# Sample attention of a hybrid decoder step: cached keys and values in ten tiles per sequence in place of twelve

## The reference, cut to what matters

```python
DILATED = ((128, 1), (512, 4), (2048, 16))

def dilated_attention_sample(q, kc, vc):          # kc, vc: 2048 cached rows, then 8 new ones
    W = kc.shape[1] - T
    for window, dil in DILATED:
        j = jnp.arange(window // dil + 1)
        idx = W + ti[:, None] - dil * j[None, :]
        ...                                       # scores, softmax, product with the values
        outs.append(o / den[..., None])
        lses.append(mx[..., 0] + jnp.log(den))
    return combine_by_denominator(outs, lses)     # weights exp(lse), so one softmax over all three sets
```

## Time and profile before

| | before |
|---|---|
| median of 3 runs | 2793.16 us (2788.93 to 2793.80) |
| span of the profiled execution | 2790.8 us |
| matrix engine busy in the span | 2667.3 us, 96% |
| VectorE, ScalarE, GpSimd busy | 65%, 39%, 25% |
| sample stage, first PE instruction to the end of its last value product | about 1077 to 1246 us |

### The profile page before, as it was taken

How to read it: one execution, slowest core, us unless ns; L and a number is a source line. 1 busy time by engine, 2 the same in 40 slices (tenths; PEclk the granted TensorE clock), 3 DMA queues, 4 the chain that set the end, 5 groups by cost and what they waited for, 6 DMA issues and landing times. The chain is left out here.

```text
span 2790.8 us, 45736 instructions
## 1 busy us (share of the span) xinstructions
PE 2667.3 (96%) x17331; PEld 2256.3 (81%) x17331; DVE 1806.6 (65%) x3848; ACT 1075.5 (39%) x1975; POOL 692.4 (25%) x585
## 2 busy tenths in 40 slices
PE   7999999999899998989989999899999999999997
PEld 6888888878777776768877888799998888778886
DVE  6722566333688885567667676755655766887778
ACT  4312332010566774333346555555553211221113
POOL 1167212120245453112210000100002434333332
PEclk9999999999999999989999999999999999999999
DMA  5367543254454547967846777778869777786672
GB/s 184 140 214 265 198 145 143 107 178 139 138 174 155 172 142 290 399 263 261 303 164 209 269 270 269 263 269 298 278 234 335 271 243 255 265 310 225 220 266 87
DMA packets 342705, 628.68 MB, mean 225 GB/s; under 512 B 38431, under 2 KB 241315, under 8 KB 326742
## 3 DMA queue, kind: packets, MB, share of 16 engines
q1 hardware_dynamic: 273132, 530.24, 54.8%
q10 hardware_dynamic: 68218, 91.51, 9.1%
q0 software_dynamic: 1152, 4.19, 0.4%
HBM read 455.36 MB, written 237.61 MB: 248 GB/s over the span
## 5 line engine op out<-in xcount | busy, mean ns | idle before, releaser
L3573 DVE TENSOR_TENSOR mlp_acc<-mlp_acc,bank 128x512 f32<-128x512 f32 x440 | 299.6, 685 | 143.4 <-PE bank L2861 137.1
L2859 PE MATMUL bank<-mlp_wd,mlp_u_hi 128*128 128x512 f32 x896 | 350.5, 391 | 8.9 <-DVE mlp_acc L3573 5.1
L2861 PE MATMUL bank<-mlp_wd,mlp_u_lo 128*128 128x512 f32 x896 | 349.2, 390 | 0.0
L2860 PE MATMUL bank<-mlp_wd,mlp_u_hi 128*128 128x512 f32 x896 | 349.1, 390 | 0.0
L3342 ACT ACTIVATE mlp_u_hi<-mlp_u_raw 128x768 fp32r<-128x768 f32 x126 | 113.1, 945 | 445.4 <-POOL mlp_u_raw L3210 445.0
L2859 PE MATMUL bank<-mlp_h_hi,mlp_wu_hi 128*128 128x272 f32 x896 | 259.3, 289 | 9.3 <-DVE mlp_h_lo L3431 4.8
L2860 PE MATMUL bank<-mlp_h_lo,mlp_wu_hi 128*128 128x272 f32 x896 | 258.8, 289 | 0.0
L2861 PE MATMUL bank<-mlp_h_hi,mlp_wu_lo 128*128 128x272 f32 x896 | 257.9, 288 | 0.0
L292 PE MATMUL p_bank<-p_w_hi,p_hT_hi 128*128 128x512 f32 x640 | 250.4, 391 | 5.2 <-DVE p_stage L836 5.1
L294 PE MATMUL p_bank<-p_w_hi,p_hT_lo 128*128 128x512 f32 x640 | 249.1, 389 | 0.0
L293 PE MATMUL p_bank<-p_w_lo,p_hT_hi 128*128 128x512 f32 x640 | 249.1, 389 | 0.0
(11 more groups left out here) (448 smaller groups left out, 6104.4 us busy)
## 6 DMA issues: line engine op xcount, KB each, us to landing
mlp_wd<-wd SPq DMA_DIRECT2D x31, 2048.0 KB, 8.1
mlp_wd<-wd SPq DMA_DIRECT2D x32, 1536.0 KB, 7.3
mlp_u_raw<-u SPq DMA_DIRECT2D x256, 128.0 KB, 2.4
out_win_k_sample<-in_cache_k SPq DMA_DIRECT2D x48, 680.0 KB, 8.9
out_win_v_sample<-in_cache_v SPq DMA_DIRECT2D x48, 680.0 KB, 9.6
mlp_wu_raw<-in_w_up SPq DMA_DIRECT2D x31, 1024.0 KB, 6.0
p_w_raw<-in_w_tok SPq DMA_DIRECT2D x10, 2048.0 KB
wd<-mlp_un_hi SPq DMA_DIRECT2D x21, 896.0 KB, 4.5
```

The costliest lines, as they stand in the source:

```text
L2859: nc.tensor.matmul(out, ah, bh, start=fresh and k == 0, stop=False, skip_group_check=not fresh)
L2860: nc.tensor.matmul(out, ah, bl, start=False, stop=False, skip_group_check=not fresh)
L2861: ins = nc.tensor.matmul(out, al, bh, start=False, stop=k == n - 1, skip_group_check=not fresh)
L3573: v.tensor_tensor(a, a, b[:], ALU.add).then_inc(summed, 1)
```

## The change

Of the last 512 rows only those of residue 8 to 15 are loaded by the second DMA, two tiles in place of four. Partition p = 32a + i gets rows 16i + 8 + 2a and the next one, counted from the start of the last 512 (2 rows, 4 KB in one run; 512 KB in all). The rows of residue 0 to 7 are there once, in the tiles of dilation 16, and the table now counts for every position all three windows. With this the third group has two tiles: two key transposes, a score block of 256 columns, two probability transposes, and the value products have 11 tiles in place of 13. All places in memory stay as large as before (`HOME`).

```diff
-KT = 13
-OLD = 12 * P
+WT = 10
+KT = WT + 1
+OLD = WT * P
 KEYS = OLD + NS
+HOME = 12
...
-    pos = np.concatenate([16 * p + r for r in range(8)] + [WB - 512 + 4 * p + c for c in range(4)]
-                         + [WB + np.arange(DEC_T)])[None, :]
+    late = WB - 512 + 16 * (p % 32) + 8 + 2 * (p // 32)
+    pos = np.concatenate([16 * p + r for r in range(8)] + [late + y for y in range(2)] + [WB + np.arange(DEC_T)])[None, :]
...
-    d16 = (back >= 0) & (back % 16 == 0) & (back <= 2048) & (part16 | new)
-    d4 = (back >= 0) & (back % 4 == 0) & (back <= 512) & ~part16
-    d1 = (back >= 0) & (back <= 128) & ~part16
+    d16 = (back >= 0) & (back % 16 == 0) & (back <= 2048)
+    d4 = (back >= 0) & (back % 4 == 0) & (back <= 512)
+    d1 = (back >= 0) & (back <= 128)
...
 def load_window(sp, dst, cache, b, landed):
     sp.dma_start(dst[:, 0:8], cache[b].rearrange("(i r) c -> i r c", r=16)[:, 0:8]).then_inc(landed, 16)
-    sp.dma_start(dst[:, 8:12], cache[b, WB - 512:WB, :].rearrange("(i r) c -> i r c", r=4)).then_inc(landed, 16)
+    sp.dma_start(dst[:, 8:WT], cache[b, WB - 512:WB, :].rearrange("(i z a y) c -> z a i y c", z=2, a=4, y=2)[1]).then_inc(landed, 16)
...
             def keys(b, ci):
-                for x in (4 * ci + 1, 4 * ci + 3):
+                for x in range(4 * ci + 1, min(4 * ci + 4, WT), 2):
...
             def masked(b, c):
-                w = 512 if c < 3 else NS
+                w = min(512, OLD - 512 * c) if c < 3 else NS
...
             def scores(b, ci):
-                w = 512 if ci < 3 else NS
+                w = min(512, OLD - 512 * ci) if ci < 3 else NS
...
                     if i < 3:
-                        for k in range(4):
+                        for k in range(min(4, WT - 4 * i)):
```

More of the change, by code:

```diff
@@ L1954, in sample_tables @@
     p = np.arange(P)
-    pos = np.concatenate([16 * p + r for r in range(8)] + [WB - 512 + 4 * p + c for c in range(4)]
-                         + [WB + np.arange(DEC_T)])[None, :]
+    late = WB - 512 + 16 * (p % 32) + 8 + 2 * (p // 32)
+    pos = np.concatenate([16 * p + r for r in range(8)] + [late + y for y in range(2)] + [WB + np.arange(DEC_T)])[None, :]
+    assert len(set(pos[0].tolist())) == pos.size
     back = WB + t - pos
     n = OLD + DEC_T
[L1959 to L1962, removed]
-    d16 = (back >= 0) & (back % 16 == 0) & (back <= 2048) & (part16 | new)
-    d4 = (back >= 0) & (back % 4 == 0) & (back <= 512) & ~part16
-    d1 = (back >= 0) & (back <= 128) & ~part16
+    assert pos.shape[1] == n
+    d16 = (back >= 0) & (back % 16 == 0) & (back <= 2048)
+    d4 = (back >= 0) & (back % 4 == 0) & (back <= 512)
+    d1 = (back >= 0) & (back <= 128)
     count = d16.astype(np.float32) + d4 + d1
@@ L1994, in __init__ @@
             if b < DEC_B:
-                order += [("k", b, x) for x in range(12)]
+                order += [("k", b, x) for x in range(WT)]
             if b:
@@ L2087, in mix_sample @@
         assert -(-nc.sbuf_base // 32) * 32 == K.front_at + 4 * TOP
-        sb("kin_home", [P, 12, AW])
-        later = [12 * AW]
+        sb("kin_home", [P, HOME, AW])
+        later = [HOME * AW]
         def front(name, *shape):
@@ L2099, in mix_sample @@
         knT = sb("knT", [P, PAIRS, NS])
-        pr = front("pr", 2, KEYS)
+        pr = front("pr", 2, HOME * P + NS)[:, :, 0:KEYS]
         qs, knew, mq, mkk, n32 = K.qs, K.knew, K.mq, K.mkk, K.n32
         qz = front("qz", DEC_B, PAIRS, QW)
-        pT = front("pT", KT, P)
+        pT = front("pT", HOME + 1, P)
         mask, mask_new = sb("mask", [P, OLD]), sb("mask_new", [P, DEC_B, NS])
@@ L2120, in mix_sample @@
         SC, PV, ML = (3, 4), 5, (6, 7)
-        pT_last = kin[1][:].rearrange("p x c -> p (x c)")[:, 12 * AW - KT * P:].rearrange("p (x r) -> p x r", r=P)
+        pT_last = kin[1][:].rearrange("p x c -> p (x c)")[:, HOME * AW - KT * P:].rearrange("p (x r) -> p x r", r=P)
         def pt(b):
-            return pT[:] if b + 1 < DEC_B else pT_last
+            return pT[:, 0:KT] if b + 1 < DEC_B else pT_last
         def pv(b):
@@ L2168, in _ @@
                 if b + 2 < DEC_B:
-                    sp.wait_ge(s["turned"], T.turned("k", b, 11))
+                    sp.wait_ge(s["turned"], T.turned("k", b, WT - 1))
                     load_k(b + 2)
@@ L2215, in _ @@
             assert own.n == 6
-            pool.wait_ge(s["turned"], T.turned("k", 0, 11))
+            pool.wait_ge(s["turned"], T.turned("k", 0, WT - 1))
             for h in range(MH):
@@ L2235, in rows @@
         def rows(x):
-            return P if x < 12 else NS
+            return P if x < WT else NS
         @block.scalar
@@ L2251, in keys @@
             def keys(b):
-                for x in range(0, 12, 2):
+                for x in range(0, WT, 2):
                     n = 3 * b + x // 4
@@ L2269, in probs @@
                         act.wait_ge(s["summed"], b)
-                    A(pt(b)[:, 4 * i:4 * i + 4], bank[T.bank("p", b, i)][:].rearrange("p (x r) -> p x r", x=4),
+                    w = min(4, WT - 4 * i)
+                    A(pt(b)[:, 4 * i:4 * i + w], bank[T.bank("p", b, i)][:, 0:w * P].rearrange("p (x r) -> p x r", x=w),
                       ACT.Copy).then_inc(s["copied_a"], 1)
@@ L2336, in masked @@
                     dve.wait_ge(s["turned"], T.turned("p", b - 2, 3))
-                table = mask[:, 512 * c:512 * (c + 1)] if c < 3 else mask_new[:, b]
-                v.tensor_tensor_reduce(pr[:, p, 512 * c:512 * c + w], bank[SC[n % 2]][:, 0:w], table, 1.0, 2 * NEG,
+                at = 512 * c if c < 3 else OLD
+                table = mask[:, at:at + w] if c < 3 else mask_new[:, b]
+                v.tensor_tensor_reduce(pr[:, p, at:at + w], bank[SC[n % 2]][:, 0:w], table, 1.0, 2 * NEG,
                                        ALU.add, ALU.max, st[:, p, c:c + 1]).then_inc(s["masked"], 1)
@@ L2465, in keys @@
                 p = b % 2
-                for x in range(4 * ci, 4 * ci + 4):
+                for x in range(4 * ci, min(4 * ci + 4, WT)):
                     dst = open_group("k", b, x)
@@ L2473, in scores @@
                 n = 4 * b + ci
-                w = 512 if ci < 3 else NS
+                w = min(512, OLD - 512 * ci) if ci < 3 else NS
                 if ci < 3:
-                    after(pe, T.out("k", b, 4 * ci + 2))
-                    after(pe, T.out("k", b, 4 * ci + 3))
+                    last = min(4 * ci + 4, WT)
+                    after(pe, T.out("k", b, last - 2))
+                    after(pe, T.out("k", b, last - 1))
                 if n >= 2:
@@ L3760, in sb @@
             return ctx.enter_context(K.nc.sbuf_tensor("shared_" + name, shape, F32))
-        K.k_first, K.k_second = K.place("k_first", 0, [P, 12, AW]), K.place("k_second", TOP, [P, 12, AW])
+        K.k_first, K.k_second = K.place("k_first", 0, [P, HOME, AW]), K.place("k_second", TOP, [P, HOME, AW])
         K.C = sb("C", [P, MH, MD + 1])
```

10 lines of the change are left out of this document (5 added, 5 removed).

## The result

The changed kernel takes 2847.33 us in the median of 4 runs (2846.64 to 2848.36), the kernel before 2791.05 us in 4 runs beside it: a ratio of 1.0214, 95% interval 1.0196 to 1.0233. That is 56 us slower, where I forecast 19.5.

A forecast was written before the change was run, and what follows sets the result against it. Matrix engine bounds the kernel; after the change transfers lead the sample stage. 13 loads x 2.7 = 35.1 us, less 12.0 slack, 1.0 idle and 2.6 back, gives 19.5; 2793.2 + 19.5 = 2812.7 us, range 2787 to 2830.

The forecast's parts named there:

- the mechanism that leads: Sample stage: second parts run on four of 16 DMA engines, so transfers lead the matrix engine; 0.70 for 2799 to 2825 us.
- the tail: Output projection behind the sample stage: starts 19.5 us later and is itself unchanged.
- that sign: In the changed profile, 512 KB parts land 5 us or more behind their 2048 KB parts, where 1024 KB took 2.5.
- the rate: Key and value loads: second part on four engines at 98 GB/s takes 5.3 us; each load grows 2.7 us, 13 loads 35.1.
- slack and idle time: Up to value load 6: 12.0 us between its landing and first use, plus 1.0 us in which the DMA engines were idle.
- C: Rival on the second parts: at 80 GB/s a load grows by 4.0 us, 36 us in all, 2830 us; chance 0.08.
- B: Rival: four engines run faster while twelve idle, second part about 3.7 us; near 2793, 2788 to 2799 us; chance 0.10.
- A: Rival: second parts spread over all 16 engines, matrix engine keeps the lead; 2782.8 us, 2776 to 2786; chance 0.12.
- the engine's saving: Matrix engine in the sample stage: 11.8 us less work, net 10.4; transposes 0.97 and value products 0.47 us a sequence.
- SP's issue: SP's queue: issuing a load grows from 0.43 to 0.68 us, under its waits of 98 us.
- From value products 6 to L1816: End of the sample stage: 7.58 us becomes 5.0, as VectorE's projection preparation is done during the wait; 2.6 us back.
- The lower clock behind a wait: Matrix engine: a lower clock after its new waits costs nothing, since it waits anyway.

The follow-up runs named there:

- 1024 KB on four engines: Kernel before the change, keeping its twelve tiles, with the second part's rows laid out so the source's outermost dimension is 4: 2960.3 us, ratio 1.0625.
- the keys alone: Changed kernel with key second parts kept at outermost dimension 4 and value second parts at outermost dimension 32: 2808.7 us, ratio 1.0086 to the kernel before.
- outermost 32: Changed kernel with partition p = 4i + a and the second part's source outermost dimension 32, not 4, in one DMA: 2773.7 us, ratio 0.9951 to the kernel before.

## Why the prediction was right and wrong

**Right:** the direction and the mechanism that leads. The second part runs on four engines (share 0.25 at 101 GB/s), the same four each time as far as the spacing of 26.5 us a sequence tells, the transfers lead, and PE waits before key transposes and value products, up to 14.5 us where I had 3 to 7. From L1816 to the products of sequence 7 the tail is unchanged, the 2.4 us between span and median held, and the DMA share of the middle is 0.73, forecast 0.6 to 0.8. SP's waits for PE before these loads are shorter, 54 us in place of 98. The trace after the change gives no landing time for these loads, so that sign is not shown; PE's waits stand for it.

**Wrong: one term of the sum, the rate.** The step reads "each load grows from 7.9 to 10.6 us, by 2.7 us". It took 24.9 GB/s for each of the four also while the other twelve work, and that from rows of DMAs that write all partitions with all engines or of four engines that work alone. What the runs showed in its place: from sequence 5 to 7 each of the four moves 2 x 262,144 bytes of keys and values a sequence in 26.5 us, 19.8 GB/s. The other doses give nearly the same: 786,432 bytes in 38.5 us with 1024 KB on four engines (20.4), 425,984 bytes in 22.6 us with the keys alone (1190.03 to 1212.59; 18.9). The 19.8 is an average. For 18 of these 53.0 us (1206 to 1212 and 1222 to 1234) the share is 0.26 to 0.27, and the four move 24 to 25 GB/s each. By an estimate from these numbers that leaves 17 GB/s for each in the other 35 us, when the rest are at work too, or 19 if the 1.24 MB are counted in that GpSimd's queue moves in the same time.

At 19.8 GB/s a load takes 13.2 us in place of 7.9, 5.3 more. In my own sum, with nothing else changed: 13 x 5.3 = 69, less 13.0 of slack and idle time, less 2.6, is 53 us. The span grew by 54.1 and the stage by 57.4. The term can also be read without a rate, from the issue of value load 0 to the landing of value load 6:

```profile
1078.34 0.58 SPq L2023 DMA_DIRECT2D sm_vin<-in_cache_v  x1
```

before, with the landing at 1204.5 as I had worked it out, and

```profile
1072.33 0.58 SPq L2023 DMA_DIRECT2D sm_vin<-in_cache_v  x1
```

after, with the landing at 1268.19: 126.2 us before, 195.9 after. That is 69.7 more where I had 35.1 less 1.0. Less the slack of 12.0, and less the 0.4 us that the path behind the landing really gave back (below), it is 57.3.

**The rivals.** C came nearest (2830 us against 2847), by luck: I priced the second part alone by 80 GB/s of four engines that have no company, but alone they run at 101; they are slow only in company, and then for the first part too. B, four engines with room, supposed that they get faster when others idle, and they get no further than the old 25. A was one pair of dimensions away: outermost 32 gives 2773.7 us, where I had 2776 to 2786. The stage is 14.8 us shorter, I had 10.4; the gap of 3.13 us at 1187.46 is down to 0.63, and the transposes behind it, 6.24 us before at a granted clock of 0.58, take 3.88 at 1.00: 4.9 us, which A named as its lower end. The row before:

```profile
1188.62 6.24 PE L2469 MATMUL bank<-ident,k_first 128*128 128x128 f32 x32
```

The rest of the engine's saving came as forecast, 1.09 us for a group of two tiles that took 2.00, and 2.39 for value products that took 2.83:

```profile
1171.16 0.42 PE L2525 MATMUL bank<-sm_vnew,sm_pT 64*32 64x128 f32 x6 [0.63 <-issue]
1171.51 3.88 PE L2471 MATMUL bank<-ident,k_first 128*128 128x128 f32 x32
...
1176.31 1.09 PE L2471 MATMUL bank<-ident,k_first 128*128 128x128 f32 x8
...
1181.66 2.39 PE L2525 MATMUL bank<-sm_vin,sm_pT 128*32 128x128 f32 x80 [0.42 <-DVE sm_pT L2368]
...
1184.34 3.88 PE L2471 MATMUL bank<-ident,k_second 128*128 128x128 f32 x32
```

These rows are of the version with outermost 32; a plain sequence is 12.8 us there (1171.51 to 1184.34), 14.3 before.

**Smaller misses.** SP's issue was to grow to 0.68 us a load "under its waits"; it grew to 16, and its waits fell to 54, though the DMA share says that this decided little. From value products 6 to L1816 I counted 5.0 us in place of 7.58, which gave 2.6 back; it is 7.15 (1268.19 to 1275.34), which gives 0.4. The products after the wait of 10.81 us take 4.50 us, at a granted clock of 0.50 from 1268 to 1273; the same group at 1233.38, behind a wait of 0.42 us and at 1.00, takes 2.39. The lower clock behind a wait, which I had called free, is not free on the last one.

## What to carry to other kernels

Before a load is rewritten, look at its two sides: the outermost dimension of the source (4 gave stretches with a DMA share of 0.25, 8 of 0.50, 32 a share of 0.96 in the middle of the stage), and the partitions that a DMA writes (18.0 GB/s for a busy engine with 32 neighbours, 24.6 with every fourth). Here both were set by the order of two letters in a `rearrange` and the table that goes with it, and were worth 73 us against an engine saving of 15. When a transfer comes to lead, don't price it at the rate of the rows in which it followed: ask first whether a share of 1.00 still means the same GB/s: here it was 398 before, and 294 at 1.02 with four DMAs on 32 neighbours each.

## What the runs showed of the hardware that I had not expected

- A DMA share is no rate. At a share of 1.00 the engines moved 398 GB/s before. With four DMAs for the second part they moved 294 when each wrote 32 neighbouring partitions and 382 when each wrote every fourth, from the same source rows.
- Five DMAs a load cost no more than two (2774.4 against 2773.7 us), at 0.6 us of SP's time for each of the four.
- SP stood at an issue for up to 16.3 us in the change and 24.6 with double the bytes in the second part, mostly 0.4 and at most 1.6 before. I read it as four engines that are behind. Shared between SP's queue and ScalarE's, the same loads took no issue over 0.64 us, and hardly another time (2843.3 against 2847.3 us).
- With four DMAs on 32 neighbours each, outermost 8 and outermost 32 differ by 1.1 us, within their spread, though outermost 8 has a stretch of 10 us with a share of 0.50: half the engines cost nothing there. With every fourth partition it was not tried.
